# First block of a hybrid decoder step: VectorE copies the gate rows before the last powers and builds two phase tables before the gates

## The reference, cut to what matters

```
proj = h @ w_in                         # q, k, v | z | beta, alpha (8 gate columns) | u
qkv  = silu(causal_short_conv(q, k, v)) # 12 row tiles of 128
beta = sigmoid(beta_raw)
g    = -exp(a_log) * softplus(alpha_raw + dt_bias)
...
lam_bar = exp(lam * dt)                 # S5: its powers 1..8, and the phases of lam_bar**(8 n)
```

## Time and profile before

| | before |
|---|---|
| median of 3 runs | 1298.97 us |
| profiled execution, its own time | 1299.72 us |
| profiled execution, span | 1298.0 us |
| PE busy | 1121.2 us (86%) |
| DVE busy | 552.8 us (43%) |
| ACT busy | 306.5 us (24%) |
| POOL busy | 230.6 us (18%) |
| mean granted clock of TensorE | 0.926 |

### The profile page before, as it was taken

The page is one execution under the profiler, slowest core; times in us unless marked ns, Lnnn a source line. Parts: engine busy times, 40 slices in busy tenths (PEclk is TensorE's granted clock), DMA queues, the critical chain, the costliest instruction groups (busy, mean ns, idle before and its releaser), DMA issues. The chain is left out here.

```text
span 1298.0 us, 15179 instructions
## 1 busy us (share of the span) xinstructions
PE 1121.2 (86%) x5094; PEld 680.7 (52%) x5095; DVE 552.8 (43%) x1238; ACT 306.5 (24%) x684; POOL 230.6 (18%) x366
## 2 busy tenths in 40 slices
PE   4899997996996899688879799996499999889876
PEld 3466664444865677577764445543244444434332
DVE  3143357275365354697732432546411111111128
ACT  5121231051113333322214222232011111101123
POOL 0100000085403334211120000102311111101050
PEclk9899999997998996888889899997699999999988
DMA  9587061011015000375517100006377565797463
GB/s 349 167 245 259 1 258 65 1 66 65 14 26 132 2 1 1 126 282 172 171 33 284 66 17 32 33 33 156 101 259 259 166 216 172 243 319 262 146 258 149
DMA packets 127007, 181.95 MB, mean 140 GB/s; under 512 B 36685, under 2 KB 80450, under 8 KB 126942
## 3 DMA queue, kind: packets, MB, share of 16 engines
q1 hardware_dynamic: 115948, 146.96, 34.1%
q0 software_dynamic: 7376, 21.59, 5.0%
q10 hardware_dynamic: 3626, 12.64, 2.4%
HBM read 131.62 MB, written 48.47 MB: 139 GB/s over the span
## 5 line engine op out<-in xcount | busy, mean ns | idle before, releaser
L2128 PE MATMUL bank<-w_out,H 128*128 x384 | 173.4, 605 | 11.3 <-DMA w_out<-in_w_up 6.4
L368 PE MATMUL bank<-hT,w_ring 128*128 128x344 f32 x576 | 170.9, 459 | 3.8 <-ACT hT L552 3.8
L368 PEld LDWEIGHTS bank<-hT,w_ring 128*128 128x128 f32 x576 | 110.5, 193 | 62.6 <-issue 6.4
L2128 PEld LDWEIGHTS bank<-w_out,H 128*128 128x128 f32 x384 | 72.9, 193 | 109.2 <-issue 109.2
L2408 PE MATMUL bank<-w_out,hT 128*128 128x512 f32 (+1 forms) x288 | 127.5, 595 | 0.5 <-DVE hT L1920 0.5
L453 PE MATMUL bank<-w_ring,hT 128*128 128x512 f32 x256 | 115.1, 606 | 8.8 <-issue 8.8
L2192 DVE TENSOR_TENSOR H<-H,bank 128x256 f32<-128x256 f32 x24 | 10.1, 420 | 248.2 <-ACT H L2163 248.2
L2112 PE MATMUL bank<-y1T,H 128*128 x192 | 91.4, 620 | 10.6 <-DVE H L2201 7.9
L453 PEld LDWEIGHTS bank<-w_ring,hT 128*128 128x128 f32 x256 | 64.4, 256 | 55.1 <-issue 41.7
L2408 PEld LDWEIGHTS bank<-w_out,hT 128*128 128x128 f32 (+1 forms) x288 | 50.1, 179 | 64.5 <-issue 63.7
L2112 PEld LDWEIGHTS bank<-y1T,H 128*128 128x128 f32 x192 | 35.5, 195 | 52.3 <-issue 52.3
(11 more groups left out here) (523 smaller groups left out, 1797.3 us busy)
## 6 DMA issues: line engine op xcount, KB each, us to landing
ys_d<-ZO SPq DMA_DIRECT2D x18, 1024.0 KB, 13.1
y1T<-in_w_down SPq DMA_DIRECT2D x16, 1024.0 KB, 5.6
w_out<-in_w_gate SPq DMA_DIRECT2D x16, 1024.0 KB, 8.1
w_out<-in_w_up SPq DMA_DIRECT2D x16, 1024.0 KB, 11.5
ys_d<-H ACTq DMA_DIRECT2D x24, 512.0 KB, 5.4
w_ring<-in_w_in SPq DMA_DIRECT2D x4, 2048.0 KB, 8.2
y1T<-in_w_ada SPq DMA_DIRECT2D x4, 2048.0 KB, 8.1
hT<-in_w_ada SPq DMA_DIRECT2D x4, 2048.0 KB, 13.0
```

The source lines that it names most:

```text
L368: mm = t.matmul(ps[3 * (m % 2) + s][:, 0:SEG], w_ring[:, q % 2, k, (m % 4) * P:(m % 4 + 1) * P], hT[:, k, s * SEG:(s + 1) * SEG], start=(k ...
L2128: mm = t.matmul(ps[2 + p][:, :], xT[p][:, k, :], wgu[:, bass.ds(buf, 1), k, :].rearrange("p o n -> p (o n)"), start=(k == 0), stop=(k == K ...
```

## The change

VectorE's list in the first block gets another order; no instruction is added or removed. The powers 6 to 8 move from behind the last convolution tile to behind the copies of the gate banks. The first two tables move from behind the wait for the gates to ahead of it, and `absx` with them from ahead of table 0 to behind table 1.

```diff
@@ -919,20 +919,19 @@
                         inputs()
                     elif m == 10:
                         powers(2, 6)
-                    elif m == 11:
-                        powers(6, LAGS + 1)
                 pe.wait(v, "gate_rows")
                 for x in range(3):
                     dve.did(v.tensor_copy(gate_rows[:, x * SEG:(x + 1) * SEG], ps[x][:, 0:SEG]), "gate_rows")
+                powers(6, LAGS + 1)
                 power_copies()
                 eighth_angle()
+                tables(0)
+                tables(1)
 
                 v.wait_ge(hp_land, 32)
                 act.wait(v, "gates")
                 dve.did(v.tensor_tensor(sp_t[:, 0], gates[:, :, 4:8], bc(hp[:, 0, :], [P, 9, HEADS], 1), ALU.add), "absx")
 
-                tables(0)
-                tables(1)
                 tables(2)
                 tables(3)
                 act.wait(v, "ln")
```

## The result

| | before | changed |
|---|---|---|
| runs of the first comparison | 1298.19 us median (1295.00 to 1302.08, 4 runs) | 1278.54 us median (1278.37 to 1280.27, 4 runs) |
| ratio | | 0.985 (95%: 0.9821 to 0.9879) |
| profiled execution, its own time | 1299.72 us | 1278.47 us |
| span | 1298.0 us | 1276.9 us |
| mean granted clock of TensorE | 0.926 | 0.933 |

The change made the kernel 19.65 us faster by the medians; 1281.7 had been predicted, in a range of 1278 to 1287.

What follows compares the result with a forecast made beforehand. TensorE was taken to pace the first block, its gaps being what can be had. 4.35 + 10.6 + 2.4 = 17.3 us off 1299.72 gives 1282.4 profiled, 0.75 above the median, so 1281.7; range 1278 to 1287.

Steps and rivals of the forecast that it cites:

- first gap: TensorE's 8.8 us between gate matmuls and `zu0`: gate copies ahead of the powers start `zu0` 4.35 us earlier.
- clock after the first gap: TensorE's low clock from `zu0` on: taken to last as long as before, 0 us, between 2.1 lost and 2.1 won.
- second gap: TensorE's 11.84 us ahead of `ss`: with two tables ahead of the gates, 10.6 us go and about 1.25 stay.
- clock after the second gap: Thin `ss` matmuls, decay and key products: of 4.1 us lost to low clock, 2.4 come back.
- The causes of the gaps: VectorE's gate copies, late behind the powers, end the 8.8 us gap; the late table store ends the 11.84 us one.
- The covers: Slack for moved work: stores land 8.5 us before `pick7`, `absx` has 18 us, `gg` comes near 287 against about 300.
- the row at 436.90: Next block: thin matmuls after a 1.61 us gap; clock low for 3.4 us, costing 1.7, taken as the model.
- Rival A: Clock stays up over the short gap ahead of `ss`: all 4.1 us return, 19.0 us gained, 1280.0 us; chance 0.23.
- the rule of the Trainium skill's page: Only idle gaps beyond a certain length lower TensorE's clock; 1.25 us is too short, so 4.1 us return, 19.0 in sum.
- Rival B: Clock stays low through `ss` and the products; both gaps shrink, nothing more: 14.95 us gained, 1284.0 us; chance 0.18.
- C: The gap ahead of `ss` stays, not being ended by the table store: only 4.35 us gained, 1294.6 us; chance 0.05.
- D: Tables beside `zu0` to `zu2` build slower, their stores delaying `ss`: slower, 1327 us at 26 us each; chance 0.02.

Runs made afterwards that it cites:

- one table: The changed kernel with table 1 moved back behind `absx`, only table 0 ahead of the gates: median 1281.94 us, ratio 0.9888 against the kernel before.
- gap filled: The changed kernel plus three unread 256-column matmuls in TensorE's gap ahead of `ss`: median 1274.24 us, ratio 0.9829 against the kernel before.
- ScalarE's copies: The changed kernel with the gate copies done by ScalarE instead of VectorE: median 1275.47 us, ratio 0.9819 against the kernel before.

## Why the prediction was right, step by step

| term | predicted | measured in the first pair of profiles |
|---|---|---|
| first gap | 4.35 us | 8.79 - 4.32 = 4.47 us |
| clock after the first gap | 0 (-2.1 to +2.1) | 16.06 - 16.52 = -0.46 us |
| second gap | 10.6 us | 11.84 - 1.24 = 10.60 us |
| clock after the second gap | 2.4 us (0 to 4.1) | 9.99 - 7.54 = 2.45 us |
| sum in the block | 17.3 us | 17.06 by the terms, 17.02 by the stretch |

**The causes of the gaps** were right, and each was shown by itself: the copies alone gave 4.62 us, the tables alone 13.07.

**The covers** held. The last store was issued at 285.49, and `pick7` set the time at 296.8. `absx` was held up as the earlier trace rows had shown for a copy (1.26 us) and was done at 259.46, 19 us ahead of ScalarE's use at 278.88. `gg` was done at 285.96, 14 us ahead of TensorE's sum at 300.05. VectorE did not become the pace either: from 305.58 on TensorE was busy 69.82 of 69.82 us.

**The clock** was the only doubtful term. After the first gap the step held in part. The prediction let the clock fall ahead of the restart, because all up to 223.0 us is unchanged. In the 4.3 us of that gap the granted clock was 0.80 in the profile shown and 0.82 with one table and with the second gap filled, but 1.00 with the copies alone and in the changed kernel's second profile. In these two it fell only behind the restart, and `zu0` and `zu1` took 15.67 us instead of 16.5 to 16.6. So the same instructions ahead do not fix when it falls; the range of -2.1 to +2.1 us covers both cases.

After the second gap the size read from the row at 436.90 came out: in the changed kernel the clock fell after a gap of 1.24 us and was low for 2 x 0.23 x 7.54 = 3.5 us (3.4 had been taken). That row is not quite the same case, though. In the 8 us ahead of 436.90 TensorE had been busy only 3.92 of 7.97 us, at full clock, while ahead of the second gap it was busy up to the gap; and around that row the clock fell in all ten profiles, behind the second gap not in all. Rival A, that it stays up over a short gap, was wrong for this profile, and with it the rule of the Trainium skill's page "TensorE: Matmul & The Clock Gate" (section "HAM oscillation — how this bites in real kernels") as the prediction had used it. Of the five profiles with that gap of 1.24 or 1.25 us and nothing in it the clock fell behind it in four (the changed kernel twice, only the tables, one table) and stayed up in one (ScalarE's copies); so A is a thing of single executions, and that the profile shown has the forecast's case is partly luck. Rival B did not occur. C and D are out: the gap went, and the four tables kept a pace of 13.0 to 13.3 us (GpSimd starts them at 233.02, 246.36, 259.36 and 272.40, and ends the last at 285.46).

**The size.** The medians fell by 19.65 us in the first comparison and by 18.25 in the second, where 17.3 was predicted; the block explains 17.0 to 17.25 in pairs of profiles. The rest is within what the later blocks vary by. So there is luck in the number too: it moved 2 us beyond the forecast's own narrow range of 1280.5 to 1283.5 and lies nearer to A's 1280.0 than to 1281.7, and only the profile shows that the block went as forecast.

Those 889 to 900 us go with TensorE's clock. Here are the two parts in which the quickest of these profiles (gap filled, the first two rows) and the longest (ScalarE's copies, the last two) differ most, the block right behind the changed one and the experts:

```profile
380.33:660.30 279.97, 229.29 (x2112) 193.86 (x2112) 169.90 (x337) 88.62 (x291) 80.05 (x136) 0.88 0.34 107
892.10:1220.50 328.40, 296.08 (x857) 140.48 (x857) 54.45 (x112) 40.12 (x83) 42.96 (x55) 0.97 0.65 217
...
373.77:660.40 286.63, 234.92 (x2112) 197.45 (x2112) 170.02 (x337) 89.15 (x292) 80.05 (x136) 0.86 0.34 105
891.90:1225.90 334.00, 301.01 (x857) 142.26 (x857) 54.48 (x113) 40.17 (x83) 43.46 (x56) 0.95 0.63 214
```

The same matmuls keep TensorE busy 5.6 and 4.9 us longer, at a lower clock. Added up behind the block in steps of 3 us, the clock was low for 135 to 160 us in the ten profiles. The time behind the block less half of that is 820.6 to 824.5 us in all ten (an estimate: at half speed half of the time is lost). Why the clock is low for longer in one execution than in another was not tried.

**A finer point missed.** The prediction treats both tables alike. One table ahead of the gates gives the same: with one, the stores land before `pick7` too.

## What to carry to other kernels

When an engine's list mixes work that others wait for with work for later, look at each long gap of the pacing engine for the instruction that ends it, and ask only how much of what stands ahead of that instruction could stand behind it. Once the next-latest wait takes over, more of the same move gives nothing (here the second table). A gap closed on TensorE also returns clock, but here only in part in four of the five profiles in which a short gap with thin matmuls was left. Real work that depends on nothing late can fill such a gap. It won its own 0.9 us here; whether it also holds the clock up is not shown.

## What the runs showed that I had not expected

- The clock behind a gap of 1.24 us followed by 2 us of thin matmuls fell in four profiles and stayed up in one with the same instructions around it. When the gap held 1.56 or 1.16 us of matmuls it stayed up, in one profile each, which is too few against the one in five to show that filling does it. Neither half alone took it down: 18 thin matmuls with no gap ahead (line 467) ran at full clock in all ten profiles, and behind a gap of 1.32 us `zu0` and `zu1` did so in both profiles that have it. Why it differs was not settled.
- The later blocks, with the same instructions in every kernel, take between 889.1 and 900.5 us. The longer ones are those in which the clock was low for longer. This can hide or double an effect of the size of the copies (4.6 us); stretches of the profile told them apart where medians of a few runs did not.
